# Re-timing a hand-woven mixer stage: dt by features, one attention step per slot, group norms apart, and an output projection that begins inside the stage

## The chip, the cores and the metric

The kernel runs on one core of one Trainium2 chip. The metric is the device time of one execution in microseconds (us), lower is better. The kernel before takes 3553.62 us, the median of three runs.

## The reference

Two networks run one after the other on 512 tokens of width 1024, in float32. The change lies in the first, which has two equal layers. One layer is a mixer, an output projection with a residual, and a gated feed-forward part:

```python
h = rms_norm(x, norm_mix_w[i])
proj = jnp.einsum("bld,de->ble", h, w_in[i])
q, k, v, z, xbc_raw, dt_raw = jnp.split(proj, split_at, axis=-1)   # dt_raw: 16 columns
...
attn_out = blocked_gqa(q, k, v)          # 8 query heads, 2 key heads, width 64
ssd_out = ssd_mixer(z, xbc_raw, dt_raw, ...)   # conv, silu, scan in 4 chunks, 8 heads, 2 directions
mixed = jnp.concatenate([attn_out, ssd_out], axis=-1)
x = x + jnp.einsum("ble,ed->bld", mixed, w_out[i])
```

In `ssd_mixer`, `dt = softplus(dt_raw + dt_bias)` sets the decays between tokens. Its result is multiplied by `silu(z)`, normalized over each of two groups of 256 features (`yg * lax.rsqrt(mean(yg * yg) + EPS)`), and scaled by `ssd_norm_w`.

## The kernel before, in words

Activations lie with features on partitions and tokens along the free dimension. A weight matrix is cut into tiles of 128 output features. `Ring` holds two of them: ScalarE writes the rounded high part (L104), VectorE the remainder (L110), and TensorE multiplies in three passes (high by high, high by low, low by high), 8 k tiles each, so 24 matmuls of 512 columns make a tile. The high part of tile n is written only when the product of tile n-2 is complete.

The mixer is `FirstMix`, called once in each of the two layers. Its work is written as strands, one per engine and purpose (projection tiles, rotary embedding, attention, state space part, norm). Each strand is a Python generator that yields a due time in slots before it issues the next piece, and `weave` issues the pieces of all strands of an engine in order of due time. A slot is half a projection tile (12 matmuls, L1542 to L1544) from tile 6 on. Every engine then runs its list strictly in order, and semaphores carry the dependencies, so a piece that waits holds everything behind it on its engine.

The parts that the change touches:

- **dt.** Tile 6 of the 19 projection tiles has 16 real columns. TensorE takes the activations as the stationary operand and the 16 weight columns as the moving one: 4 token blocks, 8 k tiles, 3 passes, 96 matmuls of 16 columns (L1528 to L1530), in two halves of 48. Their result has tokens on partitions, as the later softplus and cumulative sums want it.
- **Attention.** It has 32 steps (4 query tiles of 2 heads, 4 blocks of 128 queries), `pace` slots apart. A step is scores (L1739), turn (four transposes, L1749), mix (L1761) and for every second one a transpose back (L1768) on TensorE, with a maximum and a row scaling on VectorE and an exponential and a copy on ScalarE.
- **Heads.** After the last tile (z3) each of the 8 heads of the state space part needs in turn: decay rows by TensorE into banks 0 and 1 (L1939), an exponential on ScalarE (L2045), an addition of masks on VectorE (L2120), an exponential (L2049), a product (L2126), 28 output matmuls (L1969) and a skip connection (L2132). GpSimd adds the masks (L2202) and scales C (L2209, L2210). `silu(z)` is one ScalarE instruction with a table load (L1574).
- **Norm.** After head 7 column sums of squares for both groups (L1991) come together, then a root, a reciprocal, a spread (L1999), and per feature tile a product (L2160), a high part (L2070) and a low part (L2168).
- **Output projection.** `Residual` starts when the mixer's list has ended: 8 tiles by `Ring.products` (L122, L123, L125), k 0 to 3 from attention, k 4 to 7 from the state space part.

## Time and profile before

| what | us |
|---|---|
| median of 3 runs (3547.63 to 3556.78) | 3553.62 |
| the profiled execution's own time | 3562.29 |
| its span, first to last instruction | 3560.5 |
| TensorE busy in it (91%) | 3255.2 |
| VectorE busy (52%) | 1864.7 |
| ScalarE busy (31%) | 1111.5 |
| GpSimd busy (3%) | 100.8 |

The mean granted TensorE clock was 0.938 of full speed. The first mixer's projection tiles begin at 15.96 us and its output projection at 329.37 us; in the second layer these are 743.56 and 1053.13 us.

### The profile page before, as it was taken

How to read it: one execution, taken by the hardware profiler on the slowest of the kernel's cores; microseconds unless marked ns; L12 is line 12 of the kernel's file. 1: busy time of each engine (PE TensorE's matmuls, PEld its weight loads, DVE VectorE, ACT ScalarE, POOL GpSimd, SP SyncE). 2: the span in 40 equal slices, each digit the busy share in tenths (PEclk: the TensorE clock that was granted, in tenths of full speed). 3: DMA queues.
4: the chain of work that ended last, by engine and by line, in shares of the span. 5: the costliest groups of instructions: out<-in, count | busy, mean ns of one | idle time of the engine just before them, and what ended most of it. 6: DMA issues, size and time to landing. Idle time of an engine off the chain costs nothing. (4 is left out here: it accounts for less than half of the span.)

```text
span 3560.5 us, 40509 instructions
## 1 busy us (share of the span) xinstructions
PE 3255.2 (91%) x16358; PEld 2602.4 (73%) x16358; DVE 1864.7 (52%) x2909; ACT 1111.5 (31%) x1672; POOL 100.8 (3%) x78
## 2 busy tenths in 40 slices
PE   8988999999889999699785769999999779999998
PEld 6667888877678888588662338888888654489897
DVE  4645766756457777564455325542553223356464
ACT  3443322324433222333351013221322233333232
POOL 0021000000220000000000010000000000000000
PEclk8998999999989999899896889999999888999999
DMA  3100544521105555212100111121122010033222
GB/s 112 48 30 19 177 158 158 164 71 42 36 7 166 191 171 176 84 61 65 36 1 17 42 77 60 63 68 60 60 70 90 24 51 1 1 108 99 91 91 87
DMA packets 74230, 278.47 MB, mean 78 GB/s; under 512 B 7899, under 2 KB 12507, under 8 KB 72636
## 3 DMA queue, kind: packets, MB, share of 16 engines
q1 hardware_dynamic: 74044, 275.87, 23.5%
q8 instruction: 131, 2.15, 0.2%
q14 instruction: 55, 0.45, 0.0%
HBM read 267.45 MB, written 8.39 MB: 77 GB/s over the span
## 5 line engine op out<-in xcount | busy, mean ns | idle before, releaser
L122 PE MATMUL banks<-normed_hi,weights_hi 128*128 128x258 f32 (+2 forms) x2672 | 866.6, 340 | 27.8 <-DVE normed_lo L971 27.8
L123 PE MATMUL banks<-normed_lo,weights_hi 128*128 128x258 f32 (+2 forms) x2672 | 891.1, 339 | 0.0
L104 ACT ACTIVATE weights_hi<-weights_raw 128x1024 fp32r<-128x1024 f32 (+3 forms) x365 | 395.8, 1084 | 1284.0 <-PE banks L125 1224.2
L125 PE MATMUL banks<-normed_hi,weights_lo 128*128 128x258 f32 (+2 forms) x2672 | 745.1, 339 | 0.0
L122 PEld LDWEIGHTS banks<-normed_hi,weights_hi 128*128 128x128 f32 x2672 | 506.3, 189 | 60.6 <-DVE normed_lo L971 28.4
L110 DVE TENSOR_TENSOR weights_lo<-weights_raw,weights_hi 128x1024 fp32r<-128x1024 f32 (+3 forms) x365 | 460.3, 1261 | 172.0 <-ACT weights_hi L104 168.6
L123 PEld LDWEIGHTS banks<-normed_lo,weights_hi 128*128 128x128 f32 x2672 | 505.1, 189 | 59.4
L125 PEld LDWEIGHTS banks<-normed_hi,weights_lo 128*128 128x128 f32 x2672 | 479.3, 189 | 89.5
L123 PE MATMUL banks<-hidden_lo,weights_hi 128*128 128x512 f32 (+1 forms) x880 | 325.2, 370 | 0.0
L122 PE MATMUL banks<-hidden_hi,weights_hi 128*128 128x512 f32 (+1 forms) x880 | 316.9, 369 | 0.0
L125 PE MATMUL banks<-hidden_hi,weights_lo 128*128 128x512 f32 (+1 forms) x880 | 293.9, 366 | 0.0
L125 PEld LDWEIGHTS banks<-hidden_hi,weights_lo 128*128 128x128 f32 x880 | 165.2, 188 | 36.1
L123 PEld LDWEIGHTS banks<-hidden_lo,weights_hi 128*128 128x128 f32 x880 | 165.9, 189 | 27.4
L122 PEld LDWEIGHTS banks<-hidden_hi,weights_hi 128*128 128x128 f32 x880 | 165.8, 188 | 20.7
L654 DVE SCALAR_TENSOR_TENSOR x<-banks,modulation,x 128x256 f32<-128x256 f32 (+1 forms) x72 | 45.5, 659 | 251.1 <-PE banks L125 243.2
L1542 PE MATMUL banks<-normed_hi,weights_hi 128*128 128x512 f32 x288 | 124.4, 432 | 16.1 <-DVE weights_lo L110 16.0
L163 DVE CUSTOM_DVE_ANT_0 ada_tiles<-ada_tiles,conditions 128x1024 f32<-128x1024 f32 x96 | 117.1, 1220 | 0.0
L161 DVE CUSTOM_DVE_ANT_0 ada_products<-ada_tiles,conditions 128x1024 f32<-128x1024 f32 x96 | 117.0, 1219 | 0.0
L1543 PE MATMUL banks<-normed_lo,weights_hi 128*128 128x512 f32 x288 | 116.6, 405 | 0.0
L1544 PE MATMUL banks<-normed_hi,weights_lo 128*128 128x512 f32 x288 | 116.2, 403 | 0.0
L1796 ACT ACTIVATE probs<-banks,softmax_cols,head_scales 128x512 f32<-128x512 f32 x64 | 49.7, 777 | 199.4 <-DVE softmax_cols L1840 199.3
L1838 DVE TENSOR_REDUCE softmax_cols<-banks 128x1 f32<-128x512 f32 x64 | 44.0, 688 | 109.8 <-PE banks L1739 109.7
(364 smaller groups left out, 4345.3 us busy)
## 6 DMA issues: line engine op xcount, KB each, us to landing
weights_raw<-in_w_up SPq DMA_DIRECT2D x176, 512.0 KB, 3.5
ada_tiles<-in_ada SPq DMA_DIRECT2D x96, 512.0 KB, 3.5
weights_raw<-in_w_down SPq DMA_DIRECT2D x64, 704.0 KB, 4.0
weights_raw<-in_w_in SPq DMA_DIRECT2D x67, 512.0 KB, 3.5
weights_raw<-in_w_out SPq DMA_DIRECT2D x32, 512.0 KB, 3.5
x_kept<-x SPq DMA_DIRECT2D x2, 3072.0 KB, 10.7
x<-x_kept SPq DMA_DIRECT2D x1, 3072.0 KB, 9.9
weights_raw<-in_mla_down SPq DMA_DIRECT2D x6, 512.0 KB, 3.4
```

The source lines that it names most:

```text
L104: act.activation(self.hi[:, n % 2, 0:w], self.raw[:, n % 2, 0:w], ACT.Copy).then_inc(self.high_ready, 1)
L110: dve.tensor_tensor(self.lo[:, n % 2, 0:w], self.raw[:, n % 2, 0:w], self.hi[:, n % 2, 0:w].bitcast(F32), ALU.subtract).then_inc(self.spli ...
L122: pe.matmul(out, self.hi[:, s, m], xh, start=k == 0, stop=False)
L123: pe.matmul(out, self.hi[:, s, m], xl, start=False, stop=False)
L125: mm = pe.matmul(out, self.lo[:, s, m], xh, start=False, stop=k == kt - 1)
L161: dve.tensor_tensor_reduce(out=self.prod[:], in0=self.tile[:, a % 2], in1=self.cond[:, 0], scale=1.0, scalar=0.0, op0=ALU.mult, op1=ALU.ad ...
L163: dve.tensor_tensor_reduce(out=self.tile[:, a % 2], in0=self.tile[:, a % 2], in1=self.cond[:, 1], scale=1.0, scalar=0.0, op0=ALU.mult, op1 ...
L654: last = dve.scalar_tensor_tensor(x, ps, self.gate(j, p), x, ALU.mult, ALU.add)
L1542: pe.matmul(out, R.hi[:, s, m], hi, start=k == 0, stop=False)
L1543: pe.matmul(out, R.hi[:, s, m], lo, start=False, stop=False)
L1544: mm = pe.matmul(out, R.lo[:, s, m], hi, start=False, stop=k == KT - 1)
L1796: act.activation(self.probs[:, n % 3], self.bank(BANK_SCORES + n % 2), ACT.Exp, bias=self.sm[:, n % 4, 1:2], scale=self.scale(n), accum_ou ...
```

## The change

It alters `FirstMix` and how its output projection begins, in both layers:

1. dt is computed with its 16 features on partitions, like any other tile: 24 matmuls whose stationary operand is 16 columns wide and whose moving operand is 512 tokens. VectorE multiplies it by the norm and TensorE turns it with four transposes, into a bank from which the bias is added. The chain that follows (softplus, sums) gets later due times.
2. `pace` goes from 1.2 to 1.0 slots per attention step.
3. The first masks of GpSimd no longer wait for the last tile's evacuation, since that buffer lies elsewhere now. `silu(z)` moves from just before head 0's second exponential to just after head 1's.
4. The norm is done group by group: sums, root, reciprocal and spread of group 0 while head 7 is still at work.
5. The output projection's first two tiles are issued inside the mixer, k by k, in banks 0 and 1: k 0 to 3 of the first before head 7's outputs, of the second behind them, then k 4 and 5 of both, and k 6 and 7 of both, each when its part of the state space result is split.

```diff
@@ Line
     def bank(self, t, piece, w):
-        return self.banks[:, 2 * (t % 3) + piece, 0:w]
+        return self.banks[:, self.moved.get(t, 2 * (t % 3)) + piece, 0:w]
     def room(self, pe, t):
         if t >= 3:
-            pe.wait_ge(self.evacuated, t - 2)
+            pe.wait_ge(self.evacuated, t - 1 if t - 2 in self.moved else t - 2)
@@ Residual
-        for j in range(self.n):
+        for j in range(self.begun, self.n):
...
+    def part(self, pe, j, ks):
+        R, s = self.Z.R, (self.first + j) % 2
+        out = self.Z.bank(self.t0 + j, 0, self.segs[0][1])
+        for k in ks:
+            if j == 0:
+                self.after(pe, k)
+            (hi, lo), = self.rhs(k)
+            m = slice(k * P, (k + 1) * P)
+            pe.matmul(out, R.hi[:, s, m], hi, start=k == 0, stop=False)
+            pe.matmul(out, R.hi[:, s, m], lo, start=False, stop=False)
+            mm = pe.matmul(out, R.lo[:, s, m], hi, start=False, stop=k == KT - 1)
+        if k == KT - 1:
+            mm.then_inc(R.product, 1)
@@ FirstMix
-        self.pace = 1.2
+        self.pace = 1.0
...
+    def begin(self, out):
+        self.out, out.begun = out, 2
+        for j in range(2):
+            self.Z.moved[out.t0 + j] = j
@@ tiles_tensor
-            if name == "dt":
-                for t in range(LT):
...
-            for k in range(KT if name != "dt" else 0):
+            width = 16 if name == "dt" else P
+            for k in range(KT):
...
-                m = slice(k * P, (k + 1) * P)
+                m = slice(k * P, k * P + width)
-                pe.matmul(out, R.hi[:, s, m], hi, start=k == 0, stop=False)
+                pe.matmul(out[0:width], R.hi[:, s, m], hi, start=k == 0, stop=False)
@@ tiles_scalar
-        yield done + 0.6
+        yield self.head(1) + 0.55
         act.wait_ge(Z.evacuated, self.t0 + len(IN_TILES))
         act.activation(self.z[:], self.z[:], ACT.Silu).then_inc(on["z_silu"], 1)
@@ tiles_vector
+                self.wait(dve, "head_sums", 5)
+                dve.tensor_tensor(self.sq[0:16], ps[0:16], rstd[0:16], ALU.mult).then_inc(Z.evacuated, 1)
@@ ssd_tensor
-        yield 3.2
-        self.wait(pe, "dt_ready", 1)
+        yield 2.4
+        pe.wait_ge(Z.evacuated, self.t0 + 7)
         self.wait(pe, "q_root", 1)
         o = self.bank(BANK_AUX)
+        for t in range(LT):
+            mm = pe.transpose(o[:, 16 * t:16 * t + 16], self.sq[0:16, t * P:(t + 1) * P], K["ident"][0:16, 0:16])
+        mm.then_inc(on["dt_turned"], 1)
+        yield 3.9
+        self.wait(pe, "dt_ready", 1)
@@ norm_tensor
+        last = self.head(7)
+        yield last + 0.5
+        sums(0)
+        yield last + 1.5
+        spread(0)
+        yield last + 1.8
+        sums(1)
+        yield last + 2.4
+        spread(1)
+    def out_tensor(self, pe):
+        last = self.head(7)
+        out = self.out
+        yield last + 0.3
+        pe.wait_ge(self.Z.R.split, out.first + 1)
+        self.wait(pe, "decayed", 8)
+        self.wait(pe, "diag", 8)
+        out.part(pe, 0, range(0, 4))
+        yield last + 1.3
+        pe.wait_ge(self.Z.R.split, out.first + 2)
+        out.part(pe, 1, range(0, 4))
+        for at, ks in ((2.0, (4, 5)), (2.6, (6, 7))):
+            yield last + at
+            out.part(pe, 0, ks)
+            out.part(pe, 1, ks)
@@ ssd_pool
+        masked(0)
         pool.wait_ge(self.Z.evacuated, self.t0 + len(IN_TILES))
-        masked(0)
         masked(1)
```

How TensorE's list changes at the second half of the dt tile, before (48 such rows follow each other; `normed` is the layer's input, split in two parts):

```order
L1739 MATMUL banks<-qkv_55 128x512 [waits roped] x2
L1528 MATMUL banks<-weights_hi,normed_hi_52 128x16
L1529 MATMUL banks<-weights_lo,normed_hi_52 128x16
L1530 MATMUL banks<-weights_hi,normed_lo_53 128x16
L1528 MATMUL banks<-weights_hi,normed_hi_52 128x16
```

and with the change:

```order
L1752 MATMUL banks<-qkv_55 128x512 [waits roped] x2
L1556 MATMUL banks<-normed_hi_52,weights_hi 16x512
L1557 MATMUL banks<-normed_lo_53,weights_hi 16x512
L1558 MATMUL banks<-normed_hi_52,weights_lo 16x512
L1556 MATMUL banks<-normed_hi_52,weights_hi 16x512
```

The place among the attention's scores is the same; each half now has 12 matmuls of 512 columns where it had 48 of 16.

ScalarE's list at heads 0 and 1, before (L1574 is `silu(z)`, L2045 and L2049 a head's two exponentials, L1796 the attention's):

```order
L2045 ACTIVATE decay_rows_88<-banks 128x1024 [waits decays]
L1574 ACT_TABLE_LOAD
L1574 ACTIVATE gates_56<-gates_56 128x2048 [waits evacuated]
L1796 ACT_TABLE_LOAD [waits turned]
L1796 ACTIVATE probs_69,softmax_cols_78<-banks,softmax_cols_78,head_scales_77 128x512 [waits max]
L1803 ACTIVATE probs_t_70<-banks 128x512 [waits mixed,turned]
L2049 ACTIVATE diagonal_91<-diagonal_91 128x1024 [waits diag]
```

and with the change:

```order
L2093 ACTIVATE decay_rows_89<-banks 128x1024 [waits decays]
L1822 ACTIVATE attention_hi_59<-banks 128x128 [waits out_turned]
L2097 ACTIVATE diagonal_92<-diagonal_92 128x1024 [waits diag]
L1809 ACTIVATE probs_69,softmax_cols_78<-banks,softmax_cols_78,head_scales_77 128x512 [waits turned,max]
L1816 ACTIVATE probs_t_70<-banks 128x512 [waits mixed,turned]
L2093 ACTIVATE decay_rows_89<-banks 128x1024 [waits decays]
L2097 ACTIVATE diagonal_92<-diagonal_92 128x1024 [waits diag]
L1588 ACT_TABLE_LOAD
L1588 ACTIVATE gates_56<-gates_56 128x2048 [waits evacuated]
L1809 ACT_TABLE_LOAD [waits turned]
```

Head 0's second exponential now has no table load ahead of it; the load and `silu(z)` stand between head 1's second exponential and the attention step after it.

TensorE's list around the last head's outputs, with the change (L610 to L612 are the output projection, L2011 the sums of group 0, L1987 the outputs of head 7):

```order
L1781 MATMUL banks<-consts,out_tokens_72 128x128 [waits out_lo,token_rows]
L610 MATMUL banks<-attention_hi_59,weights_hi 128x512 [waits diag,out_lo,decayed,weights_split]
...
L612 MATMUL banks<-attention_hi_59,weights_lo 128x512
L2011 MATMUL banks<-consts,first_squares_76 128x1 [waits mix_squares,exp]
L2011 MATMUL banks<-consts,first_squares_76 128x1 x7
L1987 MATMUL banks<-diagonal_92,x_dt_62 64x128 [waits skipped,scaled_c,weights]
...
L610 MATMUL banks<-attention_hi_59,weights_hi 128x512 [waits weights_split]
...
L2021 MATMUL banks<-consts,norm_cols_87 128x128 [waits inverses]
```

Before, neither projection nor norm stood ahead of head 7's outputs, and behind them came the last attention steps. With the change every score, turn and mix stands ahead of head 6's outputs, and of all 32 scores 28 stand ahead of head 0's decay rows, where before it were 24.

## Rows read from the trace of the kernel before

**Rows 1.** Busy time by stretch of the first mixer; columns as named in the first row.
```profile
core 0: us, PE busy (x) PEld busy (x) DVE busy (x) ACT busy (x) POOL busy (x), PEclk, DMA share, GB/s
...
62.00:88.00 26.00, 24.55 (x116) 21.21 (x115) 6.03 (x10) 4.94 (x8) 0.00 (x0) 0.56 0.07 21
88.00:234.00 146.00, 139.05 (x690) 100.29 (x688) 84.68 (x167) 64.31 (x112) 12.76 (x11) 0.97 0.13 44
...
311.00:330.00 19.00, 15.11 (x92) 14.43 (x92) 8.52 (x22) 7.83 (x16) 0.00 (x0) 0.68 0.00 1
```

**Rows 2.** TensorE's timeline around the dt tile, first mixer, then second: start, duration, line.
```profile
61.90 0.17 PE L1528 MATMUL banks<-weights_hi,normed_hi 128*128 128x16 f32 x1
...
68.82 1.84 PE L1665 MATMUL banks<-consts,head_squares 128*128 128x2 f32 x8
...
76.89 0.38 PE L1528 MATMUL banks<-weights_hi,normed_hi 128*128 128x16 f32 x1
...
87.23 2.07 PE L1739 MATMUL banks<-qkv 64*128 64x512 f32 x2
...
94.19 1.12 PE L1739 MATMUL banks<-qkv 64*128 64x512 f32 x2
...
787.58 0.17 PE L1528 MATMUL banks<-weights_hi,normed_hi 128*128 128x16 f32 x1
...
818.26 1.12 PE L1739 MATMUL banks<-qkv 64*128 64x512 f32 x2
```

**Rows 3.** TensorE's timeline, one slot with an attention step.
```profile
107.58 1.12 PE L1739 MATMUL banks<-qkv 64*128 64x512 f32 x2
...
109.94 0.48 PE L1542 MATMUL banks<-normed_hi,weights_hi 128*128 128x512 f32 x1
...
112.90 0.69 PE L1739 MATMUL banks<-qkv 64*128 64x512 f32 x1
```

**Rows 4.** ScalarE's timeline at head 0.
```profile
235.71 1.28 ACT L1574 ACT_TABLE_LOAD   x1
...
238.94 1.28 ACT L1796 ACT_TABLE_LOAD   x1
...
241.48 1.05 ACT L2049 ACTIVATE diagonal<-diagonal 128x1024 f32<-128x1024 f32 x1
```

**Rows 5.** TensorE's timeline at the heads; in brackets idle time before and its releaser.
```profile
233.92 0.71 PE L1939 MATMUL banks<-sum_rows,row_select 128*128 128x512 f32 x2
...
244.26 1.09 PE L1969 MATMUL banks<-diagonal,x_dt 128*64 128x128 f32 x4 [5.41 <-DVE diagonal L2126]
...
256.44 0.86 PE L1969 MATMUL banks<-diagonal,x_dt 128*64 128x128 f32 x3 [2.34 <-DVE diagonal L2126]
...
290.41 0.72 PE L1969 MATMUL banks<-diagonal,x_dt 128*64 128x128 f32 x3 [2.36 <-DVE diagonal L2126]
...
305.81 0.65 PE L1969 MATMUL banks<-diagonal,x_dt 128*64 128x128 f32 x4 [1.56 <-DVE diagonal L2126]
...
309.01 1.12 PE L1739 MATMUL banks<-qkv 64*128 64x512 f32 x2
```

**Rows 6.** TensorE's timeline from the tail to the output projection's third tile.
```profile
311.56 1.84 PE L1991 MATMUL banks<-consts,first_squares 128*128 128x1 f32 x16
...
318.01 3.61 PE L1999 MATMUL banks<-consts,norm_cols 128*128 128x128 f32 x16
...
329.37 0.76 PE L122 MATMUL banks<-attention_hi,weights_hi 128*128 128x512 f32 x1
...
343.00 0.39 PE L122 MATMUL banks<-attention_hi,weights_hi 128*128 128x512 f32 x1
```

**Rows 7.** VectorE's timeline in the tail: one feature tile's product, another's low part.
```profile
322.38 0.74 DVE L2160 SCALAR_TENSOR_TENSOR conv<-conv,vectors,banks 128x512 f32<-128x512 f32 x1
323.04 0.69 DVE L2168 TENSOR_TENSOR ssd_lo<-conv,ssd_hi 128x512 fp32r<-128x512 f32 x1
```

**Rows 8.** ScalarE's timeline there: a feature tile's high part.
```profile
323.16 0.63 ACT L2070 ACTIVATE ssd_hi<-conv 128x512 fp32r<-128x512 f32 x1 [0.63 <-DVE conv L2160]
```

More of the change, by code:

```diff
@@ L364, in __init__ @@
         self.banks = None
+        self.moved = {}
     def take(self, name, n):
@@ L1985, in norm_tensor, with sums @@
         on, K = self.on, self.Z.K
-        yield self.tail() + 0.3
-        for g in range(2):
+        def sums(g):
+            if g == 0:
+                self.wait(pe, "exp", STEPS)
             self.wait(pe, "mix_squares", 2 * g + 2)
@@ L1990, in norm_tensor, with spread @@
                 for n in range(2):
-                    mm = pe.matmul(self.bank(7)[:, 4 * g + t:4 * g + t + 1],
+                    mm = pe.matmul(self.bank(BANK_SCORES + g)[:, t:t + 1],
                                    (self.norm_sq if g else self.sq4)[:, n, t * P:(t + 1) * P], K["ones"][:, 0:1],
                                    start=n == 0, stop=n == 1)
-        mm.then_inc(on["mix_sums"], 1)
-        yield self.tail() + 0.9
-        self.wait(pe, "inverses", 1)
-        for g in range(2):
+            mm.then_inc(on["mix_sums"], 1)
+        def spread(g):
+            self.wait(pe, "inverses", g + 1)
+            if g:
+                self.wait(pe, "token_rows", STEPS)
             for t in range(LT):
-                mm = pe.matmul(self.bank(1 - g)[:, t * P:(t + 1) * P],
+                mm = pe.matmul(self.bank(BANK_OUT if g else BANK_TURNED)[:, t * P:(t + 1) * P],
                                self.ncols[:, 4 * g + t:4 * g + t + 1].broadcast_to([P, P]), K["ident"], start=True,
@@ L2062, in norm_scalar @@
                            ACT.Square).then_inc(on["mix_squares"], 1)
-        yield self.tail() + 0.5
-        self.wait(act, "mix_sums", 1)
-        act.activation(self.ncols[:], self.bank(7)[:, 0:8], ACT.Sqrt, scale=1.0 / 256,
-                       bias=K["eps"]).then_inc(on["roots"], 1)
+            if n >= 2:
+                g = n - 2
+                yield self.head(7) + (2.1 if g else 0.7)
+                self.wait(act, "mix_sums", g + 1)
+                act.activation(self.ncols[:, 4 * g:4 * g + 4], self.bank(BANK_SCORES + g)[:, 0:4], ACT.Sqrt,
+                               scale=1.0 / 256, bias=K["eps"]).then_inc(on["roots"], 1)
         for n in range(4):
-            yield self.tail() + 1.2 + 0.2 * n
+            yield self.tail(n // 2) + 0.1 + 0.2 * (n % 2)
             self.wait(act, "finished", n + 1)
@@ L2072, in gate @@
     def gate(self, n):
-        return max(self.done(18) + 0.9 + 0.1 * n, self.head(2 * n + 1) + 2.0)
+        return self.head(2 * n + 1) + (1.5 if n == 3 else 2.0)
     def ssd_vector(self, dve):
@@ L2077, in ssd_vector @@
         step = self.chain(dve, "dt_step")
-        yield 2.4
+        yield 2.8
         bias = c("dt_bias", self.layer).unsqueeze(1).broadcast_to([P, LT, 16])
         step.step(dve.memset(self.ap[:], 0.0))
-        dve.wait_ge(Z.evacuated, self.t0 + 7)
-        step.step(dve.tensor_tensor(self.dt[:], self.dt[:], bias, ALU.add))
+        self.wait(dve, "dt_turned", 1)
+        raw = self.bank(BANK_AUX)[:, 0:64].rearrange("p (t h) -> p t h", t=LT)
+        step.step(dve.tensor_tensor(self.dt[:], raw, bias, ALU.add))
         dve.scalar_tensor_tensor(self.dta[:], self.dt[:], -1.0, self.dt[:], ALU.mult, ALU.max).then_inc(on["dt_abs"], 1)
-        yield 2.9
+        yield 3.6
         self.wait(dve, "dt_log", 3)
@@ L2152, in norm_vector @@
             dve.tensor_tensor(self.conv[:, n], self.conv[:, n], self.z[:, n], ALU.mult).then_inc(on["gated"], 1)
-        yield self.tail() + 0.7
-        self.wait(dve, "roots", 1)
-        dve.reciprocal(self.ncols[:], self.ncols[:]).then_inc(on["inverses"], 1)
+            if n >= 2:
+                g = n - 2
+                yield self.head(7) + (2.2 if g else 0.9)
+                self.wait(dve, "roots", g + 1)
+                cols = self.ncols[:, 4 * g:4 * g + 4]
+                dve.reciprocal(cols, cols).then_inc(on["inverses"], 1)
         for n in range(4):
-            yield self.tail() + 1.1 + 0.2 * n
+            yield self.tail(n // 2) + 0.2 * (n % 2)
             self.wait(dve, "spreads", n // 2 + 1)
@@ L2160, in norm_vector @@
             dve.scalar_tensor_tensor(self.conv[:, n], self.conv[:, n], c("ssd_norm_w", self.layer)[:, n:n + 1],
[L2161 to L2164 removed]
+                                     self.bank(BANK_OUT if n >= 2 else BANK_TURNED), ALU.mult,
+                                     ALU.mult).then_inc(on["finished"], 1)
+            yield self.tail(n // 2) + 0.2 * (n % 2) + 0.25
+            self.fine(dve, n)
     def fine(self, dve, n):
@@ L3011, in build @@
             mixed = Residual(Z, KT, mix.operand, X, latent, H=H, squares=True, after=mix.ready)
+            mix.begin(mixed)
             stages += [mix, mixed, Conditions(Z, ins["conditions"], 0 if layer == 0 else 4 * HALF)]
```

48 lines of the change are left out of this document (17 added, 31 removed).

## The prediction

> **What bounds the kernel now.** I read the page first (TensorE is busy 91% of the span), then the busy time by stretch of one mixer, then TensorE's timeline through that mixer, and last VectorE's, ScalarE's and GpSimd's timelines where TensorE stood idle. Outside the mixers nothing changes, so only the two mixers count; their timelines are alike within a fraction of a microsecond but for the clock in the dt part. Four stretches of a mixer behave differently.
>
> The dt part: the 48 matmuls of the first half run from 61.90 to 68.82, those of the second from 76.89 to 87.23 [rows 2]. That is 6.9 and 10.3 us for a tile that has an eighth of another's columns. The reader should see the granted clock beside it: 0.56 over this stretch [rows 1]. TensorE was at its full level (2.4 GHz) before, and fell to the lower one (1.2 GHz) while these 16-column matmuls went through it without idle time.
>
> The tile part, 88 to 234 us, is bound by TensorE: busy 139.05 of 146 us at a clock of 0.97, VectorE 84.68 [rows 1]. A slot with an attention step takes 5.32 us, from one score to the next [rows 3].
>
> The heads, 233.92 to the end of head 7's outputs at 309.01, are bound by a chain over four engines: head 0's outputs begin 10.3 us after its decay rows, head 1's 12.2 us later, and the six heads from there to head 7 take 8.2 us each [rows 5]. TensorE waits there for VectorE's product L2126, and runs at the lower level behind the longer waits: four output matmuls take 1.09 us behind 5.41 us of idle time and 0.65 us behind 1.56 us [rows 5].
>
> The tail, 309.01 to 329.37, has the last attention steps, both norms and a clock of 0.68 [rows 1, 6]. The projection's first two tiles end at 343.00 [rows 6], so from the end of the outputs to there it is 34.0 us.
>
> **dt by features.** Removed are 96 matmuls of 16 columns, added 24 of 512 columns with a 16-wide stationary operand, which no row shows. Twelve matmuls of 512 columns with a full stationary operand take 2.96 us with what surrounds them, 109.94 to 112.90 [rows 3]; I take that, 5.9 us for the tile. It could be a little less with fewer weights to load, and not more, as the same number of columns passes. What surrounds the tile, 68.82 to 76.89 and 87.23 to 94.19, is 8.1 and 7.0 us at mostly the lower level [rows 2]. Without the 16-column matmuls TensorE has no reason to leave the full level there, so I take 5.4 us (1.5 of the 8.1 is a wait for the rotary embedding, which stays) and 4.7 us. The stretch from 61.90 to 94.19, 32.3 us, becomes 16.0: **-16.3 us**. In the second mixer it is 30.7 us [rows 2], so **-14.7 us**. Bounds: -11.5 if the clock stays as it is (only 17.3 to 5.9), -18 if the wait vanishes too.
>
> Added behind it are four transposes of a 16-row block. The nearest row is the spread, eight matmuls of 128 columns in 3.61 us at the lower level [rows 6], so at most 0.9 us for four at the full one; I take 0.6. VectorE's product over 16 rows of 512 columns replaces one over 64 columns; it is hidden behind TensorE's two or three half tiles until the transposes are due. The softplus and its table load now come between two attention exponentials with less room than before: I take 1.3 us, about one load of 1.28 us [rows 4]; bounds 0 and 2.6. Together **+1.9 us** per mixer.
>
> **One attention step per slot.** Nothing is removed. Four steps more (28 scores instead of 24) lie ahead of head 0, where TensorE is the bound, so each costs its full work: a slot of 5.32 us less 12 matmuls. Without their transitions those are 2.8 us, so 2.5 us a step, **+10 us** per mixer. Below that it can't go, since there is no idle time to take them except the 7 us in waits for copies out of the shared bank, which the new order leaves about as they are. Above it is a rival, below. The steps must leave the heads and the tail to pay for this.
>
> **Heads.** In head 0 ScalarE ran two table loads and `silu(z)`, 235.71 to 240.22, ahead of the second exponential at 241.48 [rows 4]. That block moves behind head 1's second exponential. Head 0's exponential then waits for VectorE's addition alone, some 4.2 us after the decay rows, and its outputs begin 6.8 us after them instead of 10.3. Head 1 follows after 8.5 us instead of 12.2, as GpSimd's first masks are made ahead of time. Head 2 takes 9.2 us, since the 4.5 us block is now in its way and the attention's idle time on ScalarE covers all but 1 of it. Here a table load takes 1.28 us and the next instruction starts with it [rows 4]. The page "ScalarE: Activation LUTs" of the Trainium skill (section on what a table load costs) adds a drain of about 1.38 us to each switch; by it the moved block would last 2.8 us longer and head 2 with it, 5.5 us for both mixers, but the rows show no such gap. Head 3 takes 8.2 us as now. Heads 4, 5 and 6 have a turn and a mix but no score (1.05 us), and VectorE no maximum to wait for between a head's addition and its product: I take 6.6 us each, where the work of TensorE alone is about 5.4 and the old period 8.2. Head 7 has 12 projection matmuls (2.8 us) and the sums of group 0 (1.8 us by the row of 16 [rows 6]) ahead of its outputs: 8.0 us. Its outputs take 3.2 us, as 305.81 to 309.01 [rows 5]. Sum: 6.8 + 8.5 + 9.2 + 8.2 + 3 x 6.6 + 8.0 + 3.2 = 63.7 us instead of 75.1: **-11.4 us**. Bounds: -4, if only the silu block helps, and -16, if heads 4 to 6 run at TensorE's own pace.
>
> **Tail.** Behind head 7's outputs come 12 matmuls of the second tile (2.8 us), the spread of group 0 (0.9) and the sums of group 1 (1.7): 5.4 us, which cover skip, gating and square. Root and reciprocal make it 5.9. Each feature tile of a group then needs product, high part and low part in turn, 0.74 + 0.63 + 0.69 [rows 7, 8], 2.1 us. So k 4 is ready at 8.0 and k 5 at 10.1; nine matmuls behind that take 2.1 us at the full and 4.2 at the lower level, I take 13.3 for their end. Only then the spread of group 1 (0.9) is issued, since it stands behind them in TensorE's list; k 6 is ready at 16.3, k 7 at 18.4, and the two tiles end at 21.5. The third tile then waits: its high part may only be written when the first tile's product is complete, and this now comes 6 matmuls before the second tile's end instead of 24. High and low part, 1.1 and 1.3 us, less those 1.4 us, with the evacuation between them: 1.5 us. 23.0 instead of 34.0 us: **-11.0 us**. Bounds: -4 and -14.
>
> **Sum.** First mixer -16.3 + 1.9 + 10 - 11.4 - 11.0 = -26.8, second -25.2: **-52 us**. The profiled execution took 3562.29 us (1.79 beyond its span) and would take 3510; it is 8.7 us above the median of the three runs, and against that median the forecast is 3553.6 - 52 = **3502 us**. With the bounds of the terms, which won't all fall to one side, 3486 to 3520.
>
> **Rivals.**
>
> A, the tile part slows down. With a step in every slot, VectorE's taps (3.1 us a tile), evacuations and low parts delay each maximum, and TensorE waits for the exponential. For it: all engines run in order. Against it: several slots in a row have a step already and show 5.3 us, and VectorE is busy only 58% of that stretch [rows 1]. If each of 24 slots took 0.7 us more, 34 us in both mixers: 3536.
>
> B, the clock. Fewer attention steps in heads 4 to 7, and pieces of projection with waits between them, leave TensorE at the lower level: 2.4 us more for five heads' outputs and some 3 us in the tail, 15 us per mixer, 30 in all: 3532. For it: the 0.72 us for three matmuls behind 2.36 us of idle time [rows 5]. Against it: the same work lies closer together than before. "TensorE: Matmul & The Clock Gate" of the Trainium skill (section on how the oscillation bites) advises to run all k tiles ahead of a wait, which the k-by-k start does not. By that advice this piece of the change is wrong; by the rows its cost is bounded by 36 matmuls at 0.2 us more, 7.7 us per mixer.
>
> C, the early start isn't one. The low parts that k 4 to 7 need come as late as before, and the tail gains nothing but the 12 matmuls: 22 us lost, 3524. Against it: the attention's last steps no longer stand between sums and spread.
>
> D, slower. As A, but the chain over score, maximum, exponential, turn, copy, mix and row scaling (about 5.1 us end to end) with 5.1 us of VectorE's tile work put in between exceeds the two slots, 10.6 us, that two banks of scores allow. It decides from 1.3 us more per slot, 48 x 1.3 = 62 us. At 1.6 us it gives 77 us: 3579.
>
> **How the numbers follow.** Forecast 0.70, A 0.10, B 0.11, C 0.05, D 0.04. Range 3486 to 3534: it takes in the forecast's own, C and B, and leaves out D and most of A. A measurement tells 0.3%, 10.7 us, from no change. Nearly all of the first four cases lie below 3543: faster 0.92, same 0.04 (A and B together), slower 0.04 (D).
>
> **What would show it.** dt as two groups of 12 matmuls of 0.23 us each at a clock near 1.0; 5.3 us from score to score in the tile part; head 0's outputs about 7 us after its decay rows; heads 4 to 6 under 7 us; 23 us from the end of head 7's outputs to the third tile. A slot above 5.6 us, or heads 4 to 6 still at 8, would show the forecast wrong.

## The result, and the profile after it

The change measures 3533.68 us (median of 6 runs, 3524.66 to 3540.59) against 3551.72 us for the kernel before measured with it (6 runs, 3547.63 to 3556.78): a ratio of 0.9945, interval 0.9929 to 0.9961. In a second measurement it was 3529.11 against 3559.79, 0.9920 (0.9896 to 0.9943). So it is faster by 18 to 31 us, not by the 52 of the forecast. The profiled execution took 3531.66 us, 30.6 less than the one before; 26.6 of these lie ahead of the second mixer's third projection tile, the rest in code that the change doesn't touch.

The two traces agree to 0.4 us up to the first dt tile. From there the boundaries of the prediction's four stretches stand like this (us, from TensorE's timeline; "third tile" is the output projection's, and a shift of 26.6 us is reached at the one of the second mixer, 1066.67 before and 1040.11 after):

| stretch | mixer 1 before | after | moved | forecast | mixer 2 before | after | moved | forecast |
|---|---|---|---|---|---|---|---|---|
| dt part | 32.3 | 15.3 | -17.0 | -16.3 | 30.7 | 15.3 | -15.4 | -14.7 |
| tile part, to head 0's decay rows | 139.7 | 155.1 | +15.3 | +11.9 | 139.7 | 156.5 | +16.8 | +11.9 |
| heads, to the end of head 7's outputs | 75.1 | 71.4 | -3.7 | -11.4 | 74.8 | 73.0 | -1.8 | -11.4 |
| from there to the third tile | 34.0 | 23.6 | -10.4 | -11.0 | 33.9 | 23.7 | -10.2 | -11.0 |

The busy time by stretch of the first mixer, the change's counterpart to [rows 1]:

```profile
core 0: us, PE busy (x) PEld busy (x) DVE busy (x) ACT busy (x) POOL busy (x), PEclk, DMA share, GB/s
62.00:77.00 15.00, 13.14 (x60) 7.03 (x59) 7.43 (x14) 7.00 (x12) 0.00 (x0) 1.00 0.10 36
...
88.00:232.00 144.00, 135.48 (x677) 96.61 (x677) 83.62 (x166) 59.99 (x108) 14.50 (x12) 0.98 0.12 41
232.00:303.00 71.00, 55.64 (x362) 46.87 (x360) 44.33 (x60) 32.88 (x47) 27.77 (x23) 0.88 0.03 8
303.00:327.00 24.00, 18.24 (x72) 13.50 (x70) 9.26 (x14) 5.69 (x10) 0.00 (x0) 0.72 0.00 1
```

The dt part is at the full clock. In the heads TensorE is busy 55.6 of 71 us, so 15 us of waits are left; before they were 19 (55.8 busy of 75), and I expected 11 us to go.

TensorE's timeline around the dt tile, the counterpart to [rows 2]:

```profile
61.49 0.39 PE L1556 MATMUL banks<-normed_hi,weights_hi 128*16 128x512 f32 x1
...
68.42 1.13 PE L1752 MATMUL banks<-qkv 64*128 64x512 f32 x4 [1.86 <-DVE qkv L1733]
...
76.75 1.12 PE L1752 MATMUL banks<-qkv 64*128 64x512 f32 x2
...
86.16 1.08 PE L1910 MATMUL banks<-a_dt,consts 128*128 128x32 f32 x8 [1.03 <-DVE a_dt L2140]
...
88.35 0.63 PE L1556 MATMUL banks<-normed_hi,weights_hi 128*128 128x512 f32 x1
```

The tile's first 12 matmuls take 2.7 us (61.49 to 64.22) instead of the 6.9 of the first 48, and the stretch is over at 76.75. Behind it stands what I had not put down: the cumulative sums wait 1.03 us for VectorE's `a_dt`, and the next 12 matmuls run at the lower level (0.63 us each).

A slot with a step, the counterpart to [rows 3], takes 5.34 to 5.39 us:

```profile
103.83 1.12 PE L1752 MATMUL banks<-qkv 64*128 64x512 f32 x2
...
109.22 1.12 PE L1752 MATMUL banks<-qkv 64*128 64x512 f32 x2
...
114.56 1.12 PE L1752 MATMUL banks<-qkv 64*128 64x512 f32 x2
```

The heads, the counterpart to [rows 5]:

```profile
231.81 0.71 PE L1957 MATMUL banks<-sum_rows,row_select 128*128 128x512 f32 x2
...
241.82 1.08 PE L1987 MATMUL banks<-diagonal,x_dt 128*64 128x128 f32 x4 [2.21 <-issue]
...
259.09 1.11 PE L1987 MATMUL banks<-diagonal,x_dt 128*64 128x128 f32 x4 [2.91 <-DVE diagonal L2177]
...
268.08 0.65 PE L1987 MATMUL banks<-diagonal,x_dt 128*64 128x128 f32 x4 [1.11 <-DVE diagonal L2177]
...
276.23 1.11 PE L1987 MATMUL banks<-diagonal,x_dt 128*64 128x128 f32 x4 [2.65 <-DVE diagonal L2177]
...
284.70 0.65 PE L1987 MATMUL banks<-diagonal,x_dt 128*64 128x128 f32 x4 [1.67 <-DVE diagonal L2177]
```

Head 0's outputs begin 10.0 us after its decay rows (forecast 6.8), and heads 3, 4 and 5 follow after 9.0, 8.1 and 8.5 us (8.2, 6.6, 6.6). TensorE waits for the same product as before, now L2177. Why it comes late is seen on the engines behind it, at head 0 and 1. First GpSimd's and VectorE's timelines, then ScalarE's:

```profile
238.72 1.92 POOL L2256 TENSOR_TENSOR masks_minus_sums<-consts,minus_sums 128x1024 f32<-128x1024 f32 x1
...
244.95 1.00 POOL L2263 TENSOR_TENSOR scaled_c<-conv,decay_rows 128x384 f32<-128x384 f32 x1 [4.31 <-ACT decay_rows L2093]
```

```profile
239.11 2.61 DVE L2177 TENSOR_TENSOR diagonal<-diagonal,bc_scores 128x1024 f32<-128x1024 f32 x1 [0.93 <-ACT diagonal L2097]
241.64 0.68 DVE L1851 TENSOR_REDUCE softmax_cols<-banks 128x1 f32<-128x512 f32 x1
...
244.91 1.23 DVE L2171 TENSOR_TENSOR diagonal<-banks,masks_minus_sums 128x1024 f32<-128x1024 f32 x1 [1.95 <-ACT decay_rows L2093]
247.25 2.61 DVE L2177 TENSOR_TENSOR diagonal<-diagonal,bc_scores 128x1024 f32<-128x1024 f32 x1 [1.12 <-ACT diagonal L2097]
```

```profile
242.60 0.78 ACT L1809 ACTIVATE probs<-banks,softmax_cols,head_scales 128x512 f32<-128x512 f32 x1 [3.52 <-DVE softmax_cols L1853]
...
243.37 0.59 ACT L1816 ACTIVATE probs_t<-banks 128x512 f32<-128x512 f32 x1
243.85 1.02 ACT L2093 ACTIVATE decay_rows<-banks 128x1024 f32<-128x1024 f32 x1
246.17 1.06 ACT L2097 ACTIVATE diagonal<-diagonal 128x1024 f32<-128x1024 f32 x1 [1.29 <-DVE diagonal L2171]
```

Two things are to be read. **The slow product**: L2177 takes 2.61 us in heads 0 to 3 and 5 and 2.25 in head 4, where 1.22 is its usual time, and GpSimd's mask addition L2256 runs beside it each time. **The ring**: the product (239.11), the attention's maximum behind it in VectorE's list (241.64), the attention's exponential (242.60), its copy and the next head's first exponential behind that in ScalarE's list (243.85), VectorE's addition (244.91), the second exponential (246.17), and the next product (247.25). That is 8.14 us around, and TensorE's matmuls aren't in it.

The tail, the counterpart to [rows 6]:

```profile
311.53 0.80 PE L610 MATMUL banks<-ssd_hi,weights_hi 128*128 128x512 f32 x1 [2.73 <-DVE ssd_lo L2222]
...
317.28 1.05 PE L2021 MATMUL banks<-consts,norm_cols 128*128 128x128 f32 x8
...
320.56 0.79 PE L610 MATMUL banks<-ssd_hi,weights_hi 128*128 128x512 f32 x1 [2.23 <-DVE ssd_lo L2222]
...
326.81 0.63 PE L122 MATMUL banks<-attention_hi,weights_hi 128*128 128x512 f32 x1
```

It goes nearly as forecast, k 4 at 8.3 us behind the outputs (8.0) and the third tile at 23.6 (23.0), with two waits for VectorE's low parts and the lower clock behind each.

### The profile page after: what moved, and what is told of

It is laid out like the page before. It is cut to its first block and busy times, and to the rows that moved or that the text cites. A ratio compares the mean times of both kernels' runs of the same rounds, so it can differ in the third digit from the quotient of the medians.

```text
span 3529.6 us, 40247 instructions
## 1 busy us (share of the span) xinstructions
PE 3220.6 (91%) x16222; PEld 2558.0 (72%) x16222; DVE 1878.3 (53%) x2911; ACT 1113.0 (32%) x1674; POOL 97.6 (3%) x78
## 3 DMA queue, kind: packets, MB, share of 16 engines
q1 hardware_dynamic: 74044, 275.87, 23.6%
## 5 line engine op out<-in xcount | busy, mean ns | idle before, releaser
L123 PEld LDWEIGHTS banks<-normed_lo,weights_hi 128*128 128x128 f32 x2672 | 504.7, 189 | 59.4
L1556 PE MATMUL banks<-normed_hi,weights_hi 128*128 128x512 f32 (+1 forms) x304 | 131.8, 434 | 16.0 <-DVE weights_lo L110 15.9
L1557 PE MATMUL banks<-normed_lo,weights_hi 128*128 128x512 f32 (+1 forms) x304 | 123.1, 405 | 0.0
L1558 PE MATMUL banks<-normed_hi,weights_lo 128*128 128x512 f32 (+1 forms) x304 | 122.8, 404 | 0.0
```

The source lines that it names most:

```text
L123: pe.matmul(out, self.hi[:, s, m], xl, start=False, stop=False)
L1556: pe.matmul(out[0:width], R.hi[:, s, m], hi, start=k == 0, stop=False)
L1557: pe.matmul(out[0:width], R.hi[:, s, m], lo, start=False, stop=False)
L1558: mm = pe.matmul(out[0:width], R.lo[:, s, m], hi, start=False, stop=k == KT - 1)
```

## The experiments

Theory: the heads are held by the ring and by the slow product, and each can be taken away. Rivals: TensorE's own work and clock bound the heads (B); the four steps more cost the gain (pace); the early start of the projection isn't worth what it was put in for. All ratios are against runs of the kernel before that were taken with each; medians in us. These medians of the kernel before lie between 3550.54 and 3559.79, so runs that weren't taken together are better compared by their ratios.

### dt by features alone

Item 1 of the change in the kernel before; everything else as it was.

> The kernel before with dt by features alone. My theory: the dt stretch (from its first matmul to the score ahead of tile 7's second half) falls from 32.3 to about 15.3 us per mixer, as in the changed kernel, and about 2.5 us come back at the sums of dt, which are now waited for: 14 us per mixer, 3551.7 - 28 = 3524 us. Rival: the waits behind it (attention still every 1.2 slots) take back more, and it gains under 15 us in all.

Measured: 3520.49 (3517.54 to 3524.51), ratio 0.9911 (0.9894 to 0.9929). One part of the change gives 30 us, as much as the whole or more. In the first mixer its stretch measures the same 15.3 us as in the changed kernel; in the second it is 16.9, since most of the 12 matmuls of the second half ran at the lower level. Heads and tail are those of before (74.7 us, then 20.4 to the projection). So the terms on dt hold (my sum for them is 27), and items 2 to 5 together give nothing or cost up to 13 us.

### dt and the pace

```diff
-        self.pace = 1.2
+        self.pace = 1.0
@@ norm_tensor
+        self.wait(pe, "skipped", 8)
         for g in range(2):
             self.wait(pe, "mix_squares", 2 * g + 2)
```

> As dt_only, and one attention step per slot; heads, norm and projection as before (the norm's sums additionally wait for the last skip connection). Theory that a moved step is paid in full in the tile part and only partly given back by the heads: 10 us more per mixer in the tile part, 5 to 8 us less in heads, some 8 us less in the tail where the last steps stood: 0 to 12 us faster than dt_only in all, 3512 to 3524. Rival (the steps fill gaps in the heads and nothing comes back): slower than dt_only by 10 us or more.

Measured: 3529.19 (3526.01 to 3534.57), ratio 0.9937 (0.9919 to 0.9955). In its first mixer the tile part is 15.4 us longer than with dt alone (155.3 against 139.9), the heads are no shorter (75.2 us), and from their end (307.13) to the third tile (327.98) it is 20.9 us instead of 34.0; in the second these are 14.0 us longer, 73.7 and 19.5. The steps leave heads and tail: the tail gives 13.1 and 14.4 us, the heads nothing in one mixer and 1.1 us in the other. The product is part of that: it takes 2.2 to 2.6 us in five heads here (1 to 5) where with dt alone it is slow in three, in sum 3.8 us more. So the gain that I expected over dt alone (0 to 12 us) isn't there. In the traces the second mixer's projection ends at the same time, 1067.29 against 1067.16. The medians say 9 us more. Where those come from stays open; the code behind the mixers is the same, and what a single trace shows there varies by more (below).

### No early start of the projection

```diff
-            mix.begin(mixed)
...
-              self.norm_tensor(pe), self.out_tensor(pe))
+              self.norm_tensor(pe))
```

> The changed kernel with the output projection started behind the mixer, as before; all else as changed. If the early start is worth what the timeline says: tiles 1 and 2 then need 48 matmuls, 11 us, behind the last low part, against 4.2 us now; the projection's first half ahead of head 7 also fills idle time. 12 us per mixer slower minus the 2.8 us and the 1.5 us wait for weights: 5 to 9 us per mixer, 3534 + 14 = 3548. Rival: the pieces only fill time that then is missing elsewhere: under 4 us in all.

Measured: 3520.48 (3517.99 to 3529.62), ratio 0.9919 (0.9896 to 0.9943). I expected a loss of 14 us and it is no loss. The medians alone don't prove a gain: the ratio is below the changed kernel's first (0.9945) and equal to its second (0.9920). The rows do: from the end of the outputs to the third tile it takes 20.2 us (302.72 to 322.90), in the second mixer 20.2 too, where the changed kernel takes 23.6 and 23.7 (in its second trace 23.8 and 23.6). The norm by groups shows no clear gain there: 20.2 and 20.2 us against the 20.9 and 19.5 of the run before.

### GpSimd's masks behind the product

```diff
             if h >= 2:
-                self.wait(pool, "diag", h - 1)
+                self.wait(pool, "weights", h - 1)
```

> The changed kernel, GpSimd's masks for head h+2 wait for head h's product instead of head h's addition, so that they no longer run beside that product. Theory P (port): in 6 or 7 of 8 heads the product took 2.6 us instead of 1.2 beside masks of 1.9 us; without that each head is 1.4 us shorter: 9 us per mixer, 3534 - 18 = 3516. Theory L (the in-order lists of ScalarE and VectorE make a loop of which the product is one link) says the same of the product, and that a period of some 6.7 us remains. Rival: the masks then delay the next addition or slow another instruction, and under 6 us are gained.

Measured: 3525.73 (3519.61 to 3528.87), ratio 0.9923 (0.9905 to 0.9942). Every product takes 1.22 or 1.23 us now, and the heads 65.6 and 67.2 us instead of 71.4 and 73.0. The slow product is real and worth 5.8 us per mixer, not the 9 that both theories said: from head to head it is still 7 to 8 us where the attention has steps. The median lies 3 and 8 us below the changed kernel's two, which their spread doesn't make certain; the rows do.

### The changed kernel once more

> The changed kernel once more, for the spread between chips and executions. Two theories of the 9 us by which single traces differ behind the second mixer's output projection, where the code is the same (2448.7 to 2464.9 us in six traces): if it belongs to a program, this trace shows 2456.8 us there again, within 1 us, and its median is 3533 +/- 2; if it belongs to an execution, it shows another value and the median may be anywhere from 3528 to 3536.

Measured: 3529.11 (3524.07 to 3535.51), ratio 0.9920. From the last matmul of the second projection to the end its trace has 2450.7 us where the first had 2456.8. The same program differs by 6 us in code that has nothing to do with the change, so a trace's total can't judge a few microseconds; the boundaries inside the mixers can. They aren't exact either: the second mixer's heads take 71.4 us here and took 73.0, the first mixer's dt part 16.9 and 15.3; and from the dt tile to head 0's decay rows, the first mixer takes 167.5 to 171.8 us in the ten traces of kernels that share the changed kernel's order up to there.

### Each head's first exponential ahead of the attention's

```diff
         for h in range(8):
-            yield self.head(h) + 0.2
+            yield self.head(h) + (0.2 if h == 0 else -0.1)
             decay(h)
```

> The changed kernel with one edit: each head's first exponential 0.3 slots earlier, GpSimd's masks left where they were. It parts the 13 us that both edits together took off each mixer's heads (71.4 to 58.4 us; the masks' edit alone 65.6). If the ring through ScalarE's list and the slow product each cost their share: heads of about 65 us with products still at 2.6 us, time 3517. If the slow product alone is the cause and the ring follows from it: 70 us or more, time 3530.

Measured: 3516.46 (3515.51 to 3517.85), ratio 0.9893 (0.9877 to 0.9908). Heads 63.1 and 62.2 us, 8.3 and 10.8 less, though the first six products still take 2.60 or 1.95 us. That is the edit's whole effect, not the ring's alone: four of these products take 1.95 us where they took 2.61 or 2.25, so up to 2.3 us of it may be theirs.

### Both edits

> The changed kernel with two edits: GpSimd's masks of head h+2 wait for head h's product instead of its addition, and each head's first exponential is issued 0.3 slots earlier, ahead of the attention's exponential and copy. Theory of the in-order loop: the heads with a score are held by a ring through ScalarE's and VectorE's lists (product, maximum, attention exponential, copy, head exponential, addition, second exponential, product); with the head's exponential taken out of it the heads take 60 us or less (71.4 in the changed kernel, 65.6 with the masks alone moved), and the time is about 3515. Rival, TensorE's own work and its lower clock bound the heads: they stay at 64 to 66 us and the time at 3525, as with the masks alone.

Measured: 3504.24 (3500.77 to 3512.10), ratio 0.9851 (0.9825 to 0.9877). The heads take 58.4 and 59.3 us, 13.0 and 13.7 less than in the changed kernel. The time is 24.9 us below the changed kernel's second measurement, which was taken with it. VectorE's and GpSimd's timelines at heads 0 and 1:

```profile
240.34 1.22 DVE L2177 TENSOR_TENSOR diagonal<-diagonal,bc_scores 128x1024 f32<-128x1024 f32 x1 [0.92 <-ACT diagonal L2097]
...
242.72 1.22 DVE L2171 TENSOR_TENSOR diagonal<-banks,masks_minus_sums 128x1024 f32<-128x1024 f32 x1
...
245.06 1.49 DVE L2177 TENSOR_TENSOR diagonal<-diagonal,bc_scores 128x1024 f32<-128x1024 f32 x1 [1.12 <-ACT diagonal L2097]
```

```profile
241.64 1.91 POOL L2256 TENSOR_TENSOR masks_minus_sums<-consts,minus_sums 128x1024 f32<-128x1024 f32 x1 [1.63 <-DVE diagonal L2177]
...
244.46 1.01 POOL L2264 TENSOR_TENSOR scaled_c<-conv,decay_rows 128x384 f32<-128x384 f32 x1
```

The addition no longer waits for ScalarE, and from product to product it is 4.7 us here instead of 8.1. TensorE's timeline at heads 2 and 3:

```profile
255.54 0.65 PE L1987 MATMUL banks<-diagonal,x_dt 128*64 128x128 f32 x4
...
261.80 0.65 PE L1987 MATMUL banks<-diagonal,x_dt 128*64 128x128 f32 x4
```

No wait stands ahead of either, and it is 6.3 us from one to the other: TensorE's own work bounds these two heads now. Heads 4 to 6 take 6.4, 6.0 and 6.0 us, what I had forecast for them (6.6) and a bit less; head 4 still waits 1.19 us for its product. Rival B is out as a bound of the heads: at 64 to 66 us it would have stayed.

### Both edits, and no early start

> The same two edits on the changed kernel without the early start of the output projection (which measured 3520.5). If the gains add up: the heads 8 to 11 us shorter in each mixer's trace, 3520.5 - 18 = about 3503, the best version so far. If the early start was itself what the masks' edit helped: no more than 5 us, 3516.

Measured: 3493.42 (3489.91 to 3500.80), ratio 0.9821 (0.9800 to 0.9842), the lowest of all. The gains add up, and more than I wrote. TensorE's timeline behind head 7's outputs:

```profile
292.08 1.95 PE L2011 MATMUL banks<-consts,norm_squares 128*128 128x1 f32 x16 [1.22 <-ACT norm_squares L2109]
294.60 1.26 PE L2021 MATMUL banks<-consts,norm_cols 128*128 128x128 f32 x8 [0.57 <-DVE norm_cols L2209]
295.51 0.78 PE L122 MATMUL banks<-attention_hi,weights_hi 128*128 128x512 f32 x1
...
302.91 0.50 PE L122 MATMUL banks<-ssd_hi,weights_hi 128*128 128x512 f32 x1 [0.74 <-DVE ssd_lo L2222]
...
309.20 0.39 PE L122 MATMUL banks<-attention_hi,weights_hi 128*128 128x512 f32 x1
```

Both spreads stand ahead of the projection, and the first tile's k 0 to 3 cover VectorE's work on k 4 to 6. From the end of the outputs (289.78) to the third tile it is 19.4 us, in the second mixer 20.1, against 24.0 and 24.5 with the early start in the run before.

### Both edits with dt alone, the old pace and the old norm

> The kernel before with dt by features alone (3520.5) and the two edits on masks and exponentials, with its old pace, its silu(z) in head 0 and its norm. If the heads' ring is also what binds the old order: 75 us of heads become 68 or less, 3508 or less. If the attention steps that stand in the old order's heads bind: 73 to 75 us, 3517 to 3521.

Measured: 3503.11 (3499.84 to 3507.09), ratio 0.9846 (0.9827 to 0.9865). Heads 66.9 us instead of 74.7, and 66.7 in the second mixer. What the edits take away binds the old order too; its three slow products (1.95, 1.91 and 2.60 us with dt alone) are at most 2.8 of these 7.8 us, so the ring is the larger part. Against the version just above, pace, `silu(z)` and norm by groups are together worth 10 us once the ring is gone. With the ring in place they bought nothing that the medians show: the kernel without the early start, which has them, and the one with dt alone, which doesn't, measured 3520.48 and 3520.49.

### The spread of group 1 ahead of k 4 and 5

```diff
-        yield last + 2.4
+        yield last + 1.95
         spread(1)
```

On the version with both edits and the early start.

> The changed kernel with masks and exponentials moved (3504.2) and the spread of group 1 issued ahead of k 4 and 5 of the projection's first two tiles, not behind them. Theory: in the changed kernel k 6 and 7 come late because their spread stands behind matmuls that wait for VectorE; ahead of them the two waits (2.2 and 0.6 us) fall to one short one, the third tile starts 2.5 us earlier in each mixer and the time is about 3499. Rival: VectorE's own list (group 0's products and low parts first) sets when k 6 and 7 are ready, and only the wait moves: 3504.

Measured: 3497.37 (3485.18 to 3500.52), ratio 0.9832 (0.9809 to 0.9856). TensorE's timeline:

```profile
298.20 0.50 PE L610 MATMUL banks<-ssd_hi,weights_hi 128*128 128x512 f32 x1 [1.01 <-DVE ssd_lo L2222]
...
300.25 0.79 PE L610 MATMUL banks<-ssd_hi,weights_hi 128*128 128x512 f32 x1 [0.85 <-DVE ssd_lo L2222]
...
309.00 0.47 PE L122 MATMUL banks<-attention_hi,weights_hi 128*128 128x512 f32 x1 [1.19 <-DVE weights_lo L110]
```

k 6 and 7 no longer wait, and 24.0 us become 19.1 (289.89 to 309.00), in the second mixer 24.5 become 18.6, twice what I expected of it or more. This one place in TensorE's list was the early start's loss; with it mended the stretch is 0.3 and 1.5 us shorter than without an early start, though the median isn't lower. Now the third tile waits 1.19 us for its weights, near the 1.5 of my working.

### Filled

```diff
-        yield last + 1.5
+        yield last + 1.25
         spread(0)
...
-        for at, ks in ((2.0, (4, 5)), (2.6, (6, 7))):
+        for at, ks in ((2.0, (4, 5)), (2.6, (6,)), (2.7, (7,))):
```

> As the one before, and besides the spread of group 0 ahead of the second tile's k 0 to 3, so that these 12 matmuls cover VectorE's work on k 4, and k 6 and k 7 of both tiles as separate pieces. If the early start loses only by its waits and the lower clock behind them, this gets 24.1 us from the end of head 7's outputs to the third tile down to 19 or less, and the time to 3493 or less, that of the version without the early start. If pieces with waits between them lose in any order: above 3497.

Measured: 3495.14 (3491.68 to 3501.96), ratio 0.9834 (0.9811 to 0.9856). 19.7 us to the third tile in both mixers: what k 6 and 7 apart save comes back as a wait of 1.88 us for the third tile's weights, since the first tile ends nearer to the second's end. Neither expectation is met to the letter. What stands is that the order of the pieces decides what they lose, and that by the medians the best early start measured is no better than none.

### silu(z) back in head 0

On the version with both edits and without the early start.

```diff
-        yield self.head(1) + 0.55
+        yield done + 0.6
```

> The best version so far (no early start, masks and exponentials moved, 3493.4) with silu(z) back in head 0, behind its first exponential, where the kernel before had it. By my prediction's terms head 0's outputs come 3.5 us later and heads 1 and 2 lose nothing: heads 59.4 + 2 to 3.5 us, time 3498 to 3500. If the block costs the same wherever it stands in ScalarE's list: 3493.

Measured: 3501.07 (3495.90 to 3506.89), ratio 0.9850 (0.9830 to 0.9869). Head 0's outputs begin 12.0 us after the decay rows instead of 8.6, in both mixers, and the heads behind it keep their distances: 3.4 us per mixer at that point, where I had put 3.5. To the end of the heads it is 62.5 against 59.4 us in the first mixer, but 60.0 against 59.6 in the second, where the version without this edit ran head 7's outputs at the lower level.

## Why the prediction was wrong

The forecast was 52 us and the change gives 18 to 31; the traces, up to the second mixer's third tile, 26.6. The 25 us between this and the 52 lie as follows: heads 7.7 and 9.6 in the two mixers, tile part 3.4 and 4.9, tail 0.6 and 0.8, less 1.4 for dt.

- **dt, -16.3 and -14.7: right** (-17.0 and -15.4). The clock stays at 1.00 there, and that the 16-column matmuls were what took it down is borne out: half the tile is now 12 matmuls in 2.7 us, everything around it runs at the full level, and this part alone gives 30 us. It isn't at 1.00 in every execution: in 3 of the 26 mixers traced with this dt the stretch takes 16.9 us, with matmuls at 0.6 us each behind the wait for the rotary embedding.
- **+1.9 behind it and +10 for the steps: low by 3 to 5.** 11.9 became 15.3 and 16.8. The filled version, whose list is the same up to head 0, shows what of this is work and what is clock: its tile part takes 152.2 us, 12.5 more than before, of which 1.0 is the wait for `a_dt`. So the sum was near, and what the changed kernel takes beyond it is clock, in two places. Behind the `a_dt` wait the 12 matmuls cost 1.6 us more than in the filled version, which ran them at a granted clock of 1.00 behind the same 1.03 us wait. And behind a wait for `b_tokens` of 2.59 us, here in the first mixer, they cost 1.3 us more, in the second 2.7:

```profile
184.43 1.09 PE L1937 MATMUL banks<-consts,conv 128*128 128x128 f32 x4 [2.59 <-ACT b_tokens L2077]
...
185.74 0.63 PE L1557 MATMUL banks<-normed_lo,weights_hi 128*128 128x512 f32 x1
```

Rivals A and D are refuted; a slot takes 5.34 to 5.39 us, not the 6.0 of A.
- **Heads, -11.4: the step that failed** (-3.7 and -1.8). Two sentences of it are wrong. "Head 0's exponential then waits for VectorE's addition alone ... and its outputs begin 6.8 us after them": 10.0. The attention's exponential and copy stand ahead of head 0's first exponential in ScalarE's list, so this starts at 235.71, 3.9 us after the decay rows, where before it was 0.8; the second exponential comes 6.2 us after them instead of 4.2, and the product met GpSimd's mask (1.4 us). Even with both edits, which leave head 0's own exponential in its place, it is 8.6. "Heads 4, 5 and 6 have ... no score, and VectorE no maximum to wait for ...: I take 6.6 us each": 8.1, 8.5 and 6.0. These two sentences are 6.1 of the 7.7 us that the first mixer's heads miss; head 3 adds 0.8, and head 7 1.2 (9.2 for 8.0), with a wait of 1.09 us for `attention_lo` ahead of the projection's matmuls, which the sum had at nothing. I had seen that TensorE waits for VectorE's product and left open what the product waits for. I took out the delays I could name (table loads, score) and called the rest TensorE's own work, without following the ring once around. In the first mixer the masks' edit gave 5.8 us, the exponential's 8.3, both together 13.0, and with them the heads are at 58.4 us against my 63.7: this much was there to be had, but not by this order of the lists. That the kernel then stands at 3504.2 against my 3502 is luck in part, since heads better than forecast make up for the tile part.
- **The slow product was in the trace of before.** There L2126 takes 1.22 us in five heads and 1.95, 1.91 and 2.61 in heads 1, 3 and 5, each time beside L2202 (here heads 1 and 5, GpSimd and then VectorE):

```profile
253.39 1.91 POOL L2202 TENSOR_TENSOR masks_minus_sums<-consts,minus_sums 128x1024 f32<-128x1024 f32 x1 [7.43 <-DVE diagonal L2120]
255.87 1.37 POOL L2209 TENSOR_TENSOR scaled_c<-conv,decay_rows 128x384 f32<-128x384 f32 x1 [0.57 <-ACT decay_rows L2045]
...
287.37 1.91 POOL L2202 TENSOR_TENSOR masks_minus_sums<-consts,minus_sums 128x1024 f32<-128x1024 f32 x1
```

```profile
254.43 1.95 DVE L2126 TENSOR_TENSOR diagonal<-diagonal,bc_scores 128x1024 f32<-128x1024 f32 x1 [0.73 <-ACT diagonal L2049]
...
287.75 2.61 DVE L2126 TENSOR_TENSOR diagonal<-diagonal,bc_scores 128x1024 f32<-128x1024 f32 x1 [1.12 <-ACT diagonal L2049]
```

I read one duration and not how it varied: three slow products of eight before, six with the change. The pace brings heads 1 to 5: with dt and pace alone, and `silu(z)` still in head 0, these five are slow and head 0's product takes 1.23 us. With `silu(z)` and the table loads out of head 0 its second exponential follows the addition without them, and its product too comes while GpSimd is at the masks that the same addition released; in the ring this repeats head after head.
- **Tail, -11.0: right in size** (-10.4 and -10.2), and for the wrong part of the change. It is the steps that left the tail that pay, 13.1 and 14.4 us (34.0 to 20.9 and 33.9 to 19.5 with dt and the pace alone), and the norm by groups adds nothing clear (20.2 and 20.2). The early start, which I priced as part of the gain and never against the list without it, takes 3.4 us away (20.2 without, 23.6 with it). "Only then the spread of group 1 is issued, since it stands behind them in TensorE's list" was the sentence on which I should have stopped: this order costs 4.9 us by itself. That the sum came so near is luck in part: it had the end of the two tiles at 21.5 us, and it is at 23.6, with the last pieces at the lower level; and it had 1.5 us behind that for the third tile's weights, which no wait shows here.
- **Rival B, the clock**: its place was right and its rule partly. The k-by-k pieces run at the lower level behind each wait (0.63 us a matmul in 311.53 to 316). And it acts in the tile part too, where I had no term for it. The page "TensorE: Matmul & The Clock Gate" of the Trainium skill (section on how the oscillation bites) advises, for a loop of few rows that waits for DMA, to do all k tiles of a tile ahead of a wait. The version nearest to that, without the early start, is 3.4 us a mixer faster in this stretch, which agrees; but the one that keeps its pieces and orders them better gains 4.9, so the runs don't show that the pieces as such are wrong.
- **Rival C, the early start isn't one**, names what was measured of this piece, at 0.05. Its size (a tail that gains nothing) was wrong, since the steps left the tail, and its reason is half right: both pieces wait for VectorE's low parts (2.73 and 2.23 us), but the second wait goes when its spread is issued earlier.

## What to carry over

Where an engine waits for another, go on to what that one waits for, until the chain ends or closes: in lists that run strictly in order, pieces of work that have nothing to do with each other (here attention and state space part) form a ring, and its period isn't shortened by taking work off the engine that waits (with the pace alone attention steps left the heads, which took 75.2 us all the same). An instruction whose duration varies in the trace has a cause, and a change of order can make the rare case the usual one. Work that is pulled forward must be priced against the same list without it, and whatever is short and starts a long chain (here a spread of 1 us) goes ahead of it.

## What was not expected of the hardware

**VectorE's product and GpSimd.** The product ends 1.08 us after the end of the GpSimd instruction beside it, whenever this began first: 253.39 + 1.91 = 255.30 and 254.43 + 1.95 = 256.38 in the kernel before; 238.72 + 1.92 = 240.64 and 239.11 + 2.61 = 241.72 in the changed kernel; 244.46 + 1.01 = 245.47 and 245.06 + 1.49 = 246.55 with both edits. So it waits and then runs, it isn't slowed in proportion. It goes the other way too: L2209, begun at 255.87 during that product of the kernel before, takes 1.37 us instead of 1.00. VectorE's addition L2171, with one operand from the banks, keeps its 1.23 us beside L2263, and this its 1.00 (244.91 and 244.95). The page "SBUF — State Buffer" of the Trainium skill (section on who interferes with whom) says both: a VectorE instruction with two SBUF inputs contends with a GpSimd instruction that reads SBUF, the one issued first holds the shared port for its whole duration, and a VectorE instruction with a single SBUF input (outside its 2-port performance modes) doesn't contend. The traces agree.

**The granted clock isn't a function of the list alone.** Behind the same 1.03 us wait the same 12 matmuls ran at 0.63 us each in one execution and at 0.39 in another, and the part behind the mixers took 2448.7 to 2464.9 us in the traces of kernels that share it. A difference of a few microseconds between two single traces has to be pinned to rows before it is believed.
